# Moving layer 1's last adaLN products from its attention stage into layer 0's dense stage

## The chip, the cores and the metric

The kernel runs on one core of one Trainium2 chip. The metric is device time in microseconds. The core has a matrix engine (PE, TensorE), a vector engine (DVE, VectorE), a scalar engine (ACT, ScalarE), GpSimd (POOL) and a queue engine (SP) that in this kernel only issues DMAs. Each engine runs its own program in order; they meet through semaphores.

## The reference, cut to what matters

Two layers of a diffusion backbone, float32, over 256 latent and 256 context tokens of 1024 channels. Each layer takes six modulation vectors per stream out of one product, the adaLN product:

```python
def _adaln(cond, w, b):
    return jax.nn.silu(cond) @ w + b            # (1024,) @ (1024, 6144) + (6144,)

for l in range(2):
    sh1, sc1, g1, sh2, sc2, g2 = split(_adaln(c, ada_w[l], ada_b[l]), 6)      # latent stream
    csh1, csc1, cg1, csh2, csc2, cg2 = split(_adaln(c_ctx, ada_w[l], ada_b[l]), 6)   # context
    h = rms(x, norm1_w[l]) * (1 + sc1) + sh1    # and hc for the context
    ... attention, retention and convolution heads from h @ w_in[l] ...
    x = x + g1 * (concat(att, ret, cnv) @ w_out[l])
    h2 = rms(x, norm2_w[l]) * (1 + sc2) + sh2
    x = x + g2 * mixer(h2)    # layer 0: dense SwiGLU, width 2816; layer 1: top-2-of-8 experts, width 3584
```

The adaLN product depends on the conditions `c` and `c_ctx` alone, not on x, so it can be computed at any time before the vectors are used. In layer 1 the first two vectors are needed at its beginning, `g1` at its output projection, and the others behind that.

## The kernel before, in words

Matrix products of the layers are float32 accurate by three passes: a weight is split into a high and a low part in fp32r, and each product is high x high, high x low and low x high. A weight *item* of up to 1 MB is loaded by SP into one of `RAW` = 4 raw slots, ACT copies it into the high part (`split_to` on ACT, L1138), DVE subtracts for the low part (`split_to` on DVE, L1464), and PE multiplies by both (`three`, L519 to L521). A raw slot is free once DVE has made the low part (`lo_ready`); a parts slot is free once PE has used the item. The order of all loads is one list, `order_in`, built before the engines' programs and walked by SP at L1059 to L1082.

The adaLN weights are cut into 12 slices of 512 columns per layer and each slice into two halves of 1 MB, an *adaLN item*. An item is not split: `ada_product` (L525 to L538) multiplies it in plain float32 by the two conditions, in four matmuls that write four groups of 32 PSUM partitions. All products of a group of items add up in one bank. There are three groups. Group 0 (8 items, layer 0's first four slices) is multiplied at the start. Group 1 (24 items: the rest of layer 0, and layer 1's first four slices) is multiplied in layer 0's attention. Group 2 (16 items: layer 1's other eight slices) is multiplied in layer 1's attention. `ADA_ITEMS` says how many products PE does in each of the attention's iterations: for layer 1 it is 2, 3, 2, 3, 2, 2, 2 in the first seven of eight. These items are loaded into four slots, `ADA_SLOTS`: raw slots 0 and 1 and two buffers named `more`.

At the end of a group DVE copies the bank into SBUF (`ada_rows`, L1490, signals `rows_out`). PE *folds* it: eight small matmuls turn the rows into columns and add the bias (`fold_rows`, L548 and L549, signals `cols_full`). DVE copies the columns (`ada_columns`, L1495) and makes the scale of the second norm (`scale_columns`, signals `mod2_ready`). In both layers PE waits for `rows_out` at the first instruction of `project_out`, and folds after the first tile.

The attention is written as a pipeline of iterations `m` over pairs of heads: PE scores (L734), DVE masks and takes the maximum (L1706), ACT exponentials (L1215), PE transposes (L742), ACT copies (L1179), PE values (L753). DVE, ACT and GpSimd also work through the 31 taps of the convolution in it (L1692, L1202, L1440), five per iteration in layer 1.

Between the two layers stands layer 0's dense stage (`dense_ffn`), in two halves of 11 steps. Step f multiplies gate and up columns of one item (two loads of 512 KB) with all tokens: 48 matmuls of 512 columns. After the 11 steps of a half come six items of down weights. Items rotate through raw slots 0, 1, 2 and parts slots 0, 1, 2; raw slot 3 is not used there. ACT and DVE run through the same steps: in step f ACT takes the gate's activation (L1372), makes the high part of the hidden values of step f-1 (L1365), and then splits the item of step f+3; DVE likewise.

Of the kernel before, what the change touches and what calls it, by code (L numbers as in the profile page):

```python
# [28 lines left out]
RAW = 4  # L29
# [9 lines left out]
EARLY = 4  # L39
# [2 lines left out]
RO_TAP = (20, 13)  # L42
CONV_OUTS = 4
PRODUCTS = 4
ADA_ITEMS = ((2, 1, 2, 1, 2, 1, 2, 1, 2, 2, 2, 2, 2, 2, 0, 0), (2, 3, 2, 3, 2, 2, 2, 0))
ADA_SLOTS = (0, 1, RAW, RAW + 1)
TAPS = ((2, 3, 2, 3, 2, 3, 2, 3, 3, 3, 3, 2), (5, 5, 5, 5, 5, 5, 1))
READOUT = (5, 1)
# [61 lines left out]
def build(nc, io, place):  # L110
    ctx = ExitStack()
    with ctx:
# [59 lines left out]

        bank = [ctx.enter_context(nc.psum_tensor(f"bank{i}", [P, 512], F32)) for i in range(8)]
        VB, AB, OB = bank[0:4], bank[4:7], bank[7]
        rows_bank = (OB, VB[3], VB[3])

        def table(name):
            a, n = place[name]
# [102 lines left out]
        conv_full, conv_gone = sem("conv_bank_full"), sem("conv_bank_evacuated")  # L281
# [112 lines left out]
        for layer in range(DEPTH):  # L394
            if layer == 0:
                ada_items(0)
            first["in", layer] = len(items)
            n = 0
            for a, b in IN_SLICES:
                for k0, k1 in HALVES:  # L400
                    split_item([cols(io["w_in"][layer], a, b, k0, k1)], k1 - k0, b - a, n % 2, (n + layer) % 2)
                    n += 1
            ada_items(layer + 1)
            first["out", layer] = len(items)
            for h in range(2):
                for k0, k1 in HALVES:
                    split_item([cols(io["w_out"][layer], h * SLICE, (h + 1) * SLICE, k0, k1)],
                               k1 - k0, SLICE, n % 2, (n + layer) % 2)
                    n += 1
            if layer == 0:  # L410
                first["ffn"] = len(items)
                n = 0
                for p0 in range(0, FF_TILES, HALF_FF):

                    for f in range(p0, p0 + HALF_FF):
                        split_item([cols(io["ffn_w_gate"][0], f * P, (f + 1) * P), cols(io["ffn_w_up"][0], f * P, (f + 1) * P)],
                                   KT, 2 * P, n % 3, n % 3)
                        n += 1

                    for h in range(2):  # L420
                        for f0, f1 in ff_split:
                            split_item([io["ffn_w_down"][0][(p0 + f0) * P:(p0 + f1) * P, h * SLICE:(h + 1) * SLICE]
                                        .rearrange("(k p) n -> p k n", p=P)], f1 - f0, SLICE, n % 3, n % 3)
                            n += 1
                assert n % 3 == 1
# [32 lines left out]
        def _(pe):  # L458
# [93 lines left out]
            def turn_vectors():  # L552

                after(small_in, 16 * N_SMALL)
                nc.tensor.transpose(OB[:, 96:96 + 2 * KT + 2], vrows[:, :], ident[0:2 * KT + 2, 0:2 * KT + 2])\
                    .then_inc(vectors_full, 1)
# [249 lines left out]

            def project_out(layer):
                tiles = order_of(layer)
                after(rows_out)
                ring_v[0] = len(VB)  # L810
                for half in range(2):
                    outs = {}
                    for k0, k1 in HALVES:
                        n, hi, lo = next_item()
                        for i, t in enumerate(tiles):
                            if half == 0:
                                pe.wait_ge(mix_lo, mixed[layer, t, k0 // 4])
                            if t not in outs:
                                outs[t] = open_v()
                            tok = slice(t * P, (t + 1) * P)  # L820
                            for k in range(k0, k1):
                                mm = three(outs[t][:, :], (hTr[:, 0, k, tok], hTr[:, 1, k, tok]),
                                           (hi[:, k - k0, :], lo[:, k - k0, :]), k == 0, k == KT - 1)
                            if k1 == KT:
                                mm.then_inc(v_full, 1)
                            if k0 == 0 and i == len(tiles) - 1:
                                part_used(n, mm)
                            if half == 0 and k0 == 0:
                                if i == 0:
                                    after(att_read)  # L830
                                    turn_attended(layer, tiles[-1])
                                if i == len(tiles) // 2 - 1:
                                    turn_rest(layer)
                                    fold_rows(layer + 1)
                            if half == 0 and k0 and i == 0:
                                after(mod2_ready)
                                spread_gate(2, (0, 1) if layer == 0 else (0,))
                                job[("gates", layer)] = d_a[0] - 1
                    last_use[n] = (v_full, n_v[0])
                job[("mixed", layer)] = n_v[0]  # L840

            def dense_ffn():
                for p0 in range(0, FF_TILES, HALF_FF):
                    for f in range(p0, p0 + HALF_FF):
                        n, hi, lo = next_item()
                        for half in range(2):
                            b = open_a(("gate", f)) if half == 0 else open_v(("up", f))
                            c0 = half * P
                            for k in range(KT):
                                if f == 0 and half == 0 and k % (KT // 2) == 0:  # L850
                                    after(h_lo, KT // 2)
                                mm = three(b[:, :], (hi[:, k, c0:c0 + P], lo[:, k, c0:c0 + P]),
                                           (hTr[:, 0, k, :], hTr[:, 1, k, :]), k == 0, k == KT - 1)
                            mm.then_inc(a_full if half == 0 else v_full, 1)
                        last_use[n] = (v_full, n_v[0])
                    if p0 == 0:
                        spread_gate(5, (0, 1))
                        pe.wait_ge(a_done, d_a[0])
                    after(ff_lo, HALF_FF)
                    if p0:  # L860
                        turn_vectors()
                    for half in range(2):
                        outs = [open_v() for _ in range(NT)]
                        for f0, f1 in ff_split:
                            n, hi, lo = next_item()
                            for f in range(f0, f1):
                                for t in range(NT):
                                    tok = slice(t * P, (t + 1) * P)
                                    mm = three(outs[t][:, :], (HFr[:, 0, f, tok], HFr[:, 1, f, tok]),
                                               (hi[:, f - f0, :], lo[:, f - f0, :]), f == 0, f == HALF_FF - 1)  # L870
                                    if f == HALF_FF - 1:
                                        mm.then_inc(v_full, 1)
                            if f1 < HALF_FF:
                                part_used(n, mm)
                            else:
                                last_use[n] = (v_full, n_v[0])
# [173 lines left out]
        def _(sp):  # L1050
# [8 lines left out]
            for is_ada, n in order_in:  # L1059
                s = adas[n][3] if is_ada else items[n][3]  # L1060
                if is_ada and s == RAW:
                    sp.wait_ge(conv_full, CONV_OUTS * (1 if n < ADA_FIRST[2] else 2))
                if holder[s] is not None:
                    was_ada, before = holder[s]
                    sp.wait_ge(ada_used if was_ada else lo_ready, before + 1)
# [384 lines left out]
        def _(dve):  # L1450
# [228 lines left out]
            def attention(layer, base):  # L1679
# [16 lines left out]
                for m in range(last + 2):  # L1696
# [27 lines left out]
                    if m == last - 1:  # L1724
                        split_to(first["out", layer] + 2)
                    if m == last:
                        ada_rows(layer + 1)
                    if m % 4 == 1 and m >= 5:
                        turn = (m // 4 - 1) % 2
                        tile = order_of(layer)[m // 4 - 1]  # L1730
# [196 lines left out]
            for layer in range(DEPTH):  # L1927
# [22 lines left out]
                mix_low(layer, order_of(layer)[-1], 0)  # L1950
                for t in order_of(layer):
                    mix_low(layer, t, 1)
                ada_columns(layer + 1)
                scale_columns(1, mod2_ready, layer + 1)
                O = first["out", layer]
                for half in range(2):
                    split_to(O + 2 * half + 3 if half == 0 or layer == 0 else O + 4)
# [11 lines left out]
                if layer == 0:  # L1969
# [6 lines left out]
                    for p0 in range(0, FF_TILES, HALF_FF):  # L1976
# [10 lines left out]
                        hidden_low(p0 + HALF_FF - 1)  # L1987
                        if p0:
                            after(small_in, 16 * N_SMALL)
                            vectors()  # L1990
                            scale_columns(0, mod1_ready, 2)
                        for half in range(2):
                            for j in range(len(ff_split)):
                                if j == len(ff_split) - 1:
                                    for t in tiles:
                                        add_gated(half, t, p0 > 0 and half == 1)
                                n += 1
                                split_to(min(n, first["in", 1] + 2))
# [42 lines left out]
```

## Time and profile before

| | us |
|---|---|
| median of 3 runs | 2016.98 (2013.34 to 2017.33) |
| the profiled execution | 2017.29 |
| its span, first to last instruction | 2015.3 |
| PE busy | 1857.1 (92% of the span) |
| DVE busy | 1350.3 (67%) |
| ACT busy | 1036.7 (51%) |
| the chain of work that ended last, by engine | PE 78%, DVE 11%, DMA 5%, ACT 3% |

The span is one execution on one core. A busy share is an average over stages with different limits; the chain names, for each moment, the instruction that the end of the kernel stood waiting for. Layer 0's dense stage lies at about 372 to 750 us of the span, layer 1's attention at 863 to 918, and the experts from 987 to the end.

### The profile page before, as it was taken

How to read it: one execution, taken by the hardware profiler on the slowest of the kernel's cores; microseconds unless marked ns; L12 is line 12 of the kernel's file. 1: busy time of each engine (PE TensorE's matmuls, PEld its weight loads, DVE VectorE, ACT ScalarE, POOL GpSimd, SP SyncE). 2: the span in 40 equal slices, each digit the busy share in tenths (PEclk: the TensorE clock that was granted, in tenths of full speed). 3: DMA queues.
4: the chain of work that ended last, by engine and by line, in shares of the span. 5: the costliest groups of instructions: out<-in, count | busy, mean ns of one | idle time of the engine just before them, and what ended most of it. 6: DMA issues, size and time to landing. Idle time of an engine off the chain costs nothing.

```text
span 2015.3 us, 23614 instructions
## 1 busy us (share of the span) xinstructions
PE 1857.1 (92%) x8916; PEld 1499.9 (74%) x8916; DVE 1350.3 (67%) x1286; ACT 1036.7 (51%) x972; POOL 115.4 (6%) x127
## 2 busy tenths in 40 slices
PE   4899888799999987998699999999999999999997
PEld 1777457688788767857588888788887888878885
DVE  1464964432243225685698988989888888888886
ACT  2322542432122115263377776777767767667773
POOL 0021710100000000250000000000000000000000
PEclk9899989899999998998799999999999999999999
DMA  8223832432333112392499998999999999899994
GB/s 291 84 88 125 302 133 71 106 88 90 84 105 100 58 58 89 105 334 84 145 370 334 374 366 313 358 336 373 357 328 354 346 357 373 328 350 339 366 367 157
DMA packets 245914, 472.89 MB, mean 235 GB/s; under 512 B 10546, under 2 KB 60564, under 8 KB 245804
## 3 DMA queue, kind: packets, MB, share of 16 engines
q1 hardware_dynamic: 241856, 468.67, 65.5%
q10 hardware_dynamic: 3948, 2.67, 0.5%
q8 instruction: 79, 1.29, 0.3%
q14 instruction: 31, 0.25, 0.0%
HBM read 470.26 MB, written 1.05 MB: 234 GB/s over the span
## 4 chain that ended last, share of the span: by engine, by line
PE 78%; DVE 11%; DMA 5%; ACT 3%; issue 2%; POOL 1%; SPq 0%; ACTq 0%; DVEq 0%; POOLq 0%
PE bank L519 23%; PE bank L521 22%; PE bank L520 22%; DVE parts L1479 2%; DVE parts L1464 2%; PE bank L537 1%; PE bank L920 1%; DMA raw<-in_ada_w_dram 1%; PE bank L934 1%; ACT parts L1240 1%; PE bank L961 1%; DMA raw<-in_moe_w_gate_dram 1%; DMA raw<-in_moe_w_up_dram 1%; PE bank L753 1%; ACT parts L1138 1%
## 5 line engine op out<-in xcount | busy, mean ns | idle before, releaser
L1479 DVE TENSOR_TENSOR parts<-raw,parts 128x2048 fp32r<-128x2048 f32 x336 | 765.0, 2289 | 113.1 <-ACT parts L1240 112.0
L1240 ACT ACTIVATE parts<-raw 128x2048 fp32r<-128x2048 f32 x336 | 642.4, 1918 | 259.6 <-DMA raw<-in_moe_w_up_dram 90.1
L519 PE MATMUL bank<-parts,XEr 128*128 128x512 f32 x896 | 355.0, 396 | 7.7 <-DVE XEr L1479 3.9
L521 PE MATMUL bank<-parts,XEr 128*128 128x512 f32 x896 | 350.0, 391 | 0.0
L520 PE MATMUL bank<-parts,XEr 128*128 128x512 f32 x896 | 349.6, 390 | 0.0
L1138 ACT ACTIVATE parts<-raw 128x2048 fp32r<-128x2048 f32 (+1 forms) x62 | 113.3, 1831 | 331.1 <-PE bank L521 308.4
L1464 DVE TENSOR_TENSOR parts<-raw,parts 128x2048 fp32r<-128x2048 f32 (+1 forms) x62 | 135.4, 2188 | 194.1 <-ACT parts L1138 194.0
L519 PEld LDWEIGHTS bank<-parts,XEr 128*128 128x128 f32 x896 | 168.6, 188 | 43.4 <-DVE parts L1479 5.9
L521 PEld LDWEIGHTS bank<-parts,XEr 128*128 128x128 f32 x896 | 168.6, 188 | 35.8
L520 PEld LDWEIGHTS bank<-parts,XEr 128*128 128x128 f32 x896 | 168.8, 188 | 33.5
L519 PE MATMUL bank<-parts,HTr 128*128 128x512 f32 x448 | 180.8, 404 | 0.7 <-DVE parts L1479 0.7
L521 PE MATMUL bank<-parts,HTr 128*128 128x512 f32 x448 | 174.6, 390 | 0.0
L520 PE MATMUL bank<-parts,HTr 128*128 128x512 f32 x448 | 174.4, 389 | 0.0
L519 PE MATMUL bank<-hTr,parts 128*128 128x512 f32 (+1 forms) x416 | 160.7, 386 | 5.3 <-DVE parts L1464 2.1
L521 PE MATMUL bank<-hTr,parts 128*128 128x512 f32 (+1 forms) x416 | 158.6, 381 | 0.0
L520 PE MATMUL bank<-hTr,parts 128*128 128x512 f32 (+1 forms) x416 | 158.6, 381 | 0.0
L519 PE MATMUL bank<-parts,hTr 128*128 128x512 f32 (+1 forms) x320 | 124.3, 389 | 18.5 <-DVE hTr L1479 8.6
L521 PE MATMUL bank<-parts,hTr 128*128 128x512 f32 (+1 forms) x320 | 122.4, 382 | 0.0
L520 PE MATMUL bank<-parts,hTr 128*128 128x512 f32 (+1 forms) x320 | 122.2, 382 | 0.0
L1479 DVE TENSOR_TENSOR HF<-bank,SG 128x512 f32<-128x512 f32 x22 | 15.2, 692 | 145.4 <-PE bank L521 145.4
L519 PEld LDWEIGHTS bank<-parts,HTr 128*128 128x128 f32 x448 | 84.1, 188 | 22.0 <-issue 3.3
L520 PEld LDWEIGHTS bank<-parts,HTr 128*128 128x128 f32 x448 | 84.2, 188 | 20.3 <-issue 3.3
(220 smaller groups left out, 2319.0 us busy)
## 6 DMA issues: line engine op xcount, KB each, us to landing
raw<-in_moe_w_gate_dram SPq DMA_DIRECT2D x112, 1024.0 KB, 7.0
raw<-in_moe_w_up_dram SPq DMA_DIRECT2D x112, 1024.0 KB, 7.2
raw<-in_moe_w_down_dram SPq DMA_DIRECT2D x112, 1024.0 KB, 6.6
raw<-in_ada_w_dram SPq DMA_DIRECT2D x28, 1024.0 KB, 7.8
more<-in_ada_w_dram SPq DMA_DIRECT2D x20, 1024.0 KB, 7.5
raw<-in_w_in_dram SPq DMA_DIRECT2D x12, 1024.0 KB, 5.4
raw<-in_ffn_w_gate_dram SPq DMA_DIRECT2D x22, 512.0 KB, 4.0
raw<-in_ffn_w_up_dram SPq DMA_DIRECT2D x22, 512.0 KB, 5.3
```

What stands on the lines that cost most here:

```text
L519: nc.tensor.matmul(out, st[0], mv[0], start=start, stop=False)
L520: nc.tensor.matmul(out, st[0], mv[1], start=False, stop=False)
L521: return nc.tensor.matmul(out, st[1], mv[0], start=False, stop=stop)
L537: mm = nc.tensor.matmul(b[32 * j:32 * j + 32, :], cond[:, half * KT // 2 + j, c0:c0 + 32], w[:, j, :], start=opening, stop=closing)
L753: mm = nc.tensor.matmul(OB[:, head * 64:(head + 1) * 64], PT[:, n % 4, kb * P:(kb + 1) * P], proj[:, kb, C_V + 64 * g:C_V + 64 * g + 64], ...
L920: mm = nc.tensor.matmul(M[k // 4][:, (k % 4) * P:(k % 4 + 1) * P], xn[:, t, k * P:(k + 1) * P], PA[:, t, bass.ds(i * 2 + j, 1), :].rearran ...
L934: nc.tensor.matmul(M[h][:, :], SCAT[:, ee % 2, t * P:(t + 1) * P], YS[:, h * 512:(h + 1) * 512], start=True, stop=True).then_inc(scatter_f ...
L961: mm = nc.tensor.transpose(T[g % 2][:, j * P:(j + 1) * P], HE[:, g % 2, j * P:(j + 1) * P], ident)
L1138: nc.scalar.activation(parts[:, s, 0, 0:k * width], raw[:, r, 0:k * width], ACT.Copy).then_inc(hi_ready, 1)
L1240: nc.scalar.activation(parts[:, n % PARTS, 0, :], raw[:, r, :], ACT.Copy).then_inc(hi_ready, 1)
L1464: nc.vector.tensor_tensor(parts[:, s, 1, 0:k * width], raw[:, r, 0:k * width], parts_f[:, s, 0, 0:k * width], ALU.subtract).then_inc(lo_re ...
L1479: return nc.vector.tensor_tensor(out, a, b, op)
```

## The change

The 16 items of group 2 leave layer 1's attention. One stands behind each of the steps f = 2 to 17 of the dense stage, in the order of loads and in PE's program, and all go through raw slot 3. Their products add up in bank 7 (`OB`) instead of bank 3. Row copy, fold, columns and the second scale follow in the second half of the dense stage, in front of its down products.

```diff
-ADA_ITEMS = ((2, 1, 2, 1, 2, 1, 2, 1, 2, 2, 2, 2, 2, 2, 0, 0), (2, 3, 2, 3, 2, 2, 2, 0))
+ADA_ITEMS = ((2, 1, 2, 1, 2, 1, 2, 1, 2, 2, 2, 2, 2, 2, 0, 0), (0,) * 8)
+ADA_IN_FFN = range(2, 18)
-        rows_bank = (OB, VB[3], VB[3])
+        rows_bank = (OB, VB[3], OB)
   # order of loads
-            ada_items(layer + 1)
+            if layer == 0:
+                ada_items(1)
...
                         n += 1
+                        if f in ADA_IN_FFN:
+                            ada_item(1, EARLY + ADA_IN_FFN.index(f) // 2, ADA_IN_FFN.index(f) % 2, RAW - 1)
   # PE, project_out
-                after(rows_out)
+                if layer == 0:
+                    after(rows_out)
...
-                                    fold_rows(layer + 1)
+                                    if layer == 0:
+                                        fold_rows(1)
   # PE, dense_ffn
                         last_use[n] = (v_full, n_v[0])
+                        if f in ADA_IN_FFN:
+                            ada_product()
...
                     after(ff_lo, HALF_FF)
                     if p0:
+                        after(rows_out)
+                        fold_rows(2)
                         turn_vectors()
   # SP
                 if is_ada and s == RAW:
-                    sp.wait_ge(conv_full, CONV_OUTS * (1 if n < ADA_FIRST[2] else 2))
+                    sp.wait_ge(conv_full, CONV_OUTS)
+                if is_ada and n == ADA_FIRST[2]:
+                    sp.wait_ge(v_full, job[("mixed", 0)])
   # DVE, attention, project_out and the dense stage
                     if m == last:
-                        ada_rows(layer + 1)
+                        if layer == 0:
+                            ada_rows(1)
...
-                ada_columns(layer + 1)
-                scale_columns(1, mod2_ready, layer + 1)
+                if layer == 0:
+                    ada_columns(1)
+                    scale_columns(1, mod2_ready, 1)
...
                         if p0:
                             after(small_in, 16 * N_SMALL)
+                            ada_rows(2)
                             vectors()
+                            ada_columns(2)
                             scale_columns(0, mod1_ready, 2)
+                            scale_columns(1, mod2_ready, 2)
```

SP's rule for a slot stays as it is: before a load into a slot that an adaLN item holds it waits until PE has multiplied that item (`ada_used`).

## Rows read from the trace of the kernel before

**Rows 1.** Chain of waits, layer 1's attention: start us, us, what; x counts instructions
```profile
869.17 4.34 PE bank L537 x24
...
884.06 7.81 DMA more<-in_ada_w_dram
...
902.90 1.85 PE bank L537 x16
...
917.25 0.58 DVE row L1490
```

**Rows 2.** Windows, all engines: window, length, busy us (instructions) each, clock, DMA, GB/s
```profile
863.90:905.80 41.90, 38.66 (x281) 20.07 (x273) 35.88 (x79) 30.75 (x74) 26.45 (x32) 0.96 0.99 356
```

**Rows 3.** Timeline of DVE, 863 to 922: start, us, line, operation [idle before <-releaser]
```profile
887.79 0.69 DVE L1706 CUSTOM_DVE_ANT_0 SC<-bank,mask 128x512 f32<-128x512 f32 x1 [1.10 <-issue]
...
905.85 0.69 DVE L1706 CUSTOM_DVE_ANT_0 SC<-bank,mask 128x512 f32<-128x512 f32 x1 [3.53 <-PE bank L734]
...
917.16 0.66 DVE L1490 COPY row<-bank 128x512 f32<-128x512 f32 x1
...
920.89 0.69 DVE L1479 TENSOR_TENSOR proj<-bank,rsum 128x512 f32<-128x512 f32 x1
```

**Rows 4.** Timeline of ACT, end of layer 1's attention
```profile
909.88 3.70 ACT L1138 ACTIVATE parts<-raw 128x2048 fp32r<-128x2048 f32 x2
```

**Rows 5.** Timeline of PE, layer 1's attention and output projection
```profile
867.83 1.34 PE L742 MATMUL bank<-const,SC 128*128 128x128 f32 x8 [1.98 <-ACT SC L1215]
...
923.16 0.83 PE L721 MATMUL bank<-const,proj 128*128 128x128 f32 x4
...
924.71 0.29 PE L548 MATMUL bank<-const,row 128*128 128x16 f32 x2
...
926.86 0.47 PE L549 MATMUL bank<-const,biasr 24*128 24x16 f32 x2
```

**Rows 6.** Windows of three microseconds: second to last columns clock, DMA share, GB/s
```profile
870.00:873.00 3.00, 3.00 (x24) 0.68 (x16) 2.89 (x4) 3.00 (x9) 2.46 (x4) 0.59 0.50 136
...
683.00:686.00 3.00, 2.74 (x7) 2.22 (x8) 0.56 (x3) 0.00 (x0) 0.00 (x0) 0.50 0.70 212
```

**Rows 7.** Timelines of ACT, then DVE, in two steps of the dense stage
```profile
392.39 1.92 ACT L1138 ACTIVATE parts<-raw 128x2048 fp32r<-128x2048 f32 x1 [4.38 <-PE bank L521]
...
403.27 1.92 ACT L1138 ACTIVATE parts<-raw 128x2048 fp32r<-128x2048 f32 x1 [4.38 <-PE bank L521]
...
394.34 2.29 DVE L1464 TENSOR_TENSOR parts<-raw,parts 128x2048 fp32r<-128x2048 f32 x1 [0.72 <-ACT parts L1138]
```

**Rows 8.** L1076, first loads of step 6: issues, and time from issue to landing
```profile
L1076 SPq DMA_DIRECT2D raw<-in_ffn_w_gate_dram x1: 367/367/367, 385.8 to 385.8; - x1
L1076 SPq DMA_DIRECT2D raw<-in_ffn_w_up_dram x1: 585/585/585, 386.2 to 386.2; - x1
...
DMA to landing us min/median/max: 4.0/4.6/5.2
```

**Rows 9.** SP's timeline 346 to 350, then L1076's landings from 347.2 to 350
```profile
346.47 0.37 SPq L1076 DMA_DIRECT2D raw<-in_ffn_w_gate_dram  x1
...
348.69 1.57 SPq L1076 DMA_DIRECT2D raw<-in_ffn_w_up_dram  x1
...
DMA to landing us min/median/max: 5.3/6.5/7.1
```

**Rows 10.** L1068, 835 to 870: landing of adaLN items; then a window in the experts
```profile
DMA to landing us min/median/max: 5.1/5.4/7.6
...
1000.00:1050.00 50.00, 50.00 (x227) 41.35 (x226) 42.62 (x24) 38.67 (x27) 0.00 (x0) 1.00 0.90 335
```

**Rows 11.** Timeline of PE, ends of the dense stage's two halves
```profile
490.05 3.96 PE L803 MATMUL bank<-const,ada 128*128 128x128 f32 x32
494.69 0.50 PE L519 MATMUL bank<-parts,HFr 128*128 128x512 f32 x1 [0.69 <-ACT gb L1179]
...
683.26 0.29 PE L555 MATMUL bank<-const,vrows 18*128 18x18 f32 x1 [4.03 <-DVE HFr L1479]
```

## The prediction, made before the changed kernel was run

> **What bounds the kernel now.** I read the page first: PE is busy for 92% of the span and carries 78% of the chain, so PE time added where PE never idles is paid in full. Next I read the chain inside layer 1's attention, where the change takes work away. It names the adaLN products seven times, 24 records in 4.34 us first and 16 in 1.85 us last, 12.0 us in sum over the seven pieces, and one DMA wait of 7.81 us for adaLN weights [rows 1]. Read alone, this says that products and loads hold the attention by 19.8 us. So the third view was DVE's timeline there, because a chain shows one of several ways that end together. Of the 41.9 us from DVE's first mask to its last, DVE is busy 35.9 [rows 2], and only two idle pieces in it are longer than 0.1 us: 1.10 and 3.53 us [rows 3]; the rest of the difference is latency between dependent taps. From 864 to 887 it never stops. The products fill PE's gaps under DVE's work. Last I read the dense stage. A step repeats every 10.88 us (ACT's splits at 392.39 and 403.27, [rows 7]), which is 48 matmuls without a gap between them: there PE alone sets the time. The change moves work from under DVE's cover to where nothing covers it.
>
> **The products, added.** 16 products of 4 matmuls. Two products (16 records) take 1.85 us of chain [rows 1], so 0.93 each at the full clock. In the dense stage each stands alone between fp32r matmuls, and I take 1.0: 16.0 us. Below, 0.93 each gives 14.9. Above, 0.3 for the two changes of form around each gives 20.8.
> The Trainium skill (TensorEngine Tiling (Array Packing), Key Properties) says that changing the tiling mode drains TensorE, which speaks against products scattered one by one, since there are 32 changes where attention had fewer. The trace has two products in 1.85 us with such changes at both ends, so a drain can't be large there; the upper bound above already holds one.
>
> **The weights of the dense stage, late.** This is the term that the PE rows do not show. In the order of loads an adaLN item now follows the items of f = 2 to 17, all in slot 3, so SP waits before each for the product before it. Everything behind it in SP's program waits too. The adaLN item behind load f waits for the product behind step f-1; load f+1 stands behind it. So load n is issued only after step n-2 and its product, where before it was issued once the low part of item n-3 was made (SP at 385.77 for item 6, just after DVE's split in step 0) [rows 8]. Held loads are 4 to 10, the first down item, and 13 to 18; loads 11 and 12 are issued during the down products.
> From the end of that product to the item being ready: SP 0.05; the adaLN item and then 1 MB of gate and up. Gate and up alone land 5.6 us after the first issue (0.4 between the issues, then 5.2) [rows 8]. One MB more in front takes 3.1 us at 335 GB/s [rows 10], so 8.7; the adaLN issue is itself hidden, and I take 8.6. Then 0.1 to wake ACT, its split 1.92, DVE's 2.29 [rows 7], 0.1 of semaphores. Sum 13.06. Until PE needs the item it has one step and one product, 10.88 + 1.0 = 11.88. The item is 1.2 us late. A late item n delays step n, and load n+2 hangs on step n's product, so the lateness returns every second step: steps 4, 6, 8, 10 and 13, 15, 17, seven times, 8.1 us. Bounds of the landing: 6.0, as if the adaLN MB did not delay the other (nothing late, 0 us), and 9.3, from four loads of 512 KB issued at 346.47 to 348.69, the last landing 7.1 after its issue [rows 9], other small loads among them (1.9 late, 13 us).
> The Trainium skill (DMA: Bandwidth & Descriptors, Measured) gives 6.15 us for a DMA of 1 MB. By it two would take 12.3 us, the item would come 4.9 us late and the sum would grow by 26 us. The adaLN items here land within 5.1 us of issue, issue and latency included [rows 10], so I don't follow it.
>
> **Between the halves.** Before, PE starts the down products 4.64 us after the last step of the first half (490.05 to 494.69), most of it the gate spreading [rows 11]. Now ACT and DVE are behind, since in step 8 both were blocked for the first down item until about 10 and 12.5 us after the product of step 9. From there DVE has three hidden products and low parts (0.7 us each), and two more splits (2.3 and 1.8): the last low part is there at about 20 us, that is 8.0 after the end of step 10 (10.88 + 1.2 after the same product). Against 4.64 + 1.0 this is 2.4 more. PE idles over 3 us in it. After the idle of 4.03 us at 679 [rows 11] the clock stood at 0.50 [rows 6], and some matmuls at half rate add 0.6. I take 3.0; bounds 0 and 6.
>
> **Second half: rows and fold.** PE waits at 683.26 for DVE's last low part [rows 11]. Now DVE copies the rows next (0.66) [rows 3] and PE folds, eight matmuls from 924.71 to 927.33, 2.6 us less 0.3 of overlap [rows 5]. 0.7 + 2.3 + 0.3 for a longer cold start is 3.3; bounds 2.6 and 4.5. DVE's column copies and scales, under 1 us, lie under the down products. The queue past them is free: no load waits there.
> Sum added: 16.0 + 8.1 + 3.0 + 3.3 = 30.4 us.
>
> **Layer 1's attention, removed.** Without products the scores of a pair come as soon as values are done. DVE's wait of 1.10 goes. Of the 3.53 most goes, but next come ACT's taps and copies, and GpSimd's last tap, which ended 0.2 us before PE turned the convolution; I let the whole pipeline come 3.1 earlier at ACT's split, now at 909.88 [rows 4]. That split (3.70) and DVE's (4.49) remain. The row copy before the attended tile's scaling (0.66) goes. PE no longer waits for the rows, so its first tile starts some 5 us earlier, but its next instruction needs DVE's scaling at 920.89 [rows 3]: what is late next is that DVE chain, 3.1 + 0.66 + the POOL wait unchanged. So the turn at 923.16 [rows 5] comes about 4.5 earlier, since 0.9 of PE's own time stood between. The fold's 2.3 go, but 0.5 returns as the wait for the next tile's low part, which the fold hid. 4.5 + 1.8 = 6.3. Against that, PE is left with under two thirds of its work in the attention, and there it already fell to 0.59 of full clock at 870, after 1.98 us of idle before 867.83 [rows 5, 6]. At half rate PE has about 7.6 us of work per iteration (scores, turns, values at twice their 3.8) against DVE's 6.2, so it can push for a stretch: 1.0 back. Gain 5.3; bounds 0 and 9. The loads of the output weights no longer stand behind adaLN loads, but their split stands at a fixed place in ACT's program, so this is worth nothing. The DMA traffic moved is hidden in either place except as priced above.
>
> **Sum.** 30.4 - 5.3 = +25.1 against the profiled execution's 2017.29 (span 2015.3 and 2.0 around it): 2042.4. The profiled execution lies 0.3 above the median of 2016.98, so I predict 2042.
>
> **Rivals.**
> A, the chain is right (faster). Attention gives back all that the chain names: 19.8, the row copy 0.6 and the fold 2.3, 22.7 us. The dense stage costs only its lower bounds, 14.9 + 2.6 = 17.5, because loads are still in time: 5.2 less than the median, 2011.8. It decides if attention gives over 17.5 us plus whatever the loads are late. For it speaks the 7.81 us DMA wait, against it the unbroken DVE timeline before it.
> B, loads in time, but attention held by DVE. The landing is under 7.4 us after SP is released, so the item is ready before PE; then 16.0 + 3.3 + 0 to 2 between the halves, less 5.3: 2031. For it speak 4.0 us for 512 KB alone; against it 335 GB/s as the rate of a stream.
> C, loads later and the clock lost. Landing 9.3 (13 us), products at 1.2 (19), between halves 5, second half 4.5, and PE's halved clock makes it the limit of the attention, eight iterations of 1.4 us more, which eats the gain: 41.5 - 0, 2058.
> D, the change does nothing that can be told: dense PE time has slack I don't see, or gains equal costs, 2017. Against it: PE without a gap in the step.
>
> **How the numbers follow.** Forecast 0.46 (2035 to 2050), A 0.09, B 0.24, C 0.17, D 0.04. Within 0.2% (4 us), about what a measurement of this kernel can tell, holds D and the near part of A: same 0.05. Faster 0.08. Slower 0.87. The range for 8 in 10 leaves out A and D (0.13) and the far part of C: 2025 to 2057. The bounds of the terms alone, all low, 14.9 + 0 + 0 + 2.6 - 9, give +8.5, and all high 20.8 + 13 + 6 + 4.5 - 0, +44.3.
>
> **What would show it.** In the changed profile: products in the dense stage at 0.9 to 1.1 us each and full clock. SP's gate loads each issued within 0.1 us behind a product, from load 4 on. ACT's splits in the dense stage waiting for a DMA instead of for PE, and PE waiting about 1.2 us for DVE's low part in every second step (steps 4, 6, 8, 10). A longer idle of PE before the first down products. A fold between 680 and 720. In layer 1's attention no L537, DVE nearly unbroken over some 38 us, and the clock partly at half. It would be wrong if dense steps with a product stayed at 11.9 us throughout (then B), or if the attention from first scores to the first output matmul shrank by more than 10 us (then towards A).

## The result and the profile after

The changed kernel takes 2055.83 us (2051.45 to 2057.43, 4 runs) against 2017.15 us for the kernel before: ratio 1.0192, 95% interval 1.0171 to 1.0213, slower. Forecast were 2042, in a range of 2025 to 2057. The time lies at the upper end of the range, outside the 2035 to 2050 that the forecast itself stood for, and nearer to rival C (2058). The direction and the places were right, the terms of cost were too small.

The profiled execution has a span of 2054.7 us, 39.4 more than before. Cut at the same events in both traces, it comes from here:

| stretch | before | after | difference |
|---|---|---|---|
| start to the dense stage's first step | 372.96 | 371.63 | -1.3 |
| steps 0 to 10 | 117.1 | 136.2 | +19.2 |
| end of step 10 to the first down matmul | 4.6 | 7.7 | +3.1 |
| down products and steps 11 to 21 | 184.5 | 202.0 | +17.4 |
| end of step 21 to the first down matmul | 4.3 | 9.1 | +4.9 |
| down products to DVE's first mask in layer 1 | 180.5 | 180.3 | -0.2 |
| first mask to ACT's split of the output weights | 45.9 | 46.2 | +0.3 |
| that split to DVE's last normalised tile | 43.6 | 38.6 | -5.0 |
| the rest | 1061.8 | 1063.0 | +1.1 |

Experiments are read in the same cuts; the expert stage alone differs by 1 us and more between executions of equal code (1027.0 to 1035.2 us from its first gather in the profiles of this study), so small differences of totals say little, and the cuts before it say more.

The term that no PE row of before showed is there. This is the chain of waits of the changed kernel from the product behind step 2 on (start us, us, what):

```profile
401.84 1.04 PE bank L541 x8
402.90 0.37 SPq L1080
403.31 0.51 SPq L1088
403.87 8.82 DMA raw<-in_ffn_w_up_dram
412.71 1.93 ACT parts L1150
414.66 2.30 DVE parts L1476
```

SP's load of the adaLN item goes out 0.02 us after the product ends, the gate and up loads of step 4 behind it, and they land 9.8 us after that first issue; over the 13 held loads of gate and up it is 9.2 to 10.2 us until ACT starts on them. Before, ACT's split of that item had begun at 392.39 [rows 7]. ACT's row of the changed kernel says what it waited for now (columns as in [rows 7]), and PE's rows what that costs:

```profile
412.71 1.92 ACT L1150 ACTIVATE parts<-raw 128x2048 fp32r<-128x2048 f32 x1 [26.03 <-DMA raw<-in_ffn_w_up_dram]
```
```profile
401.77 1.06 PE L541 MATMUL bank<-raw,cond 128*32 128x512 f32 x8
413.88 1.07 PE L541 MATMUL bank<-raw,cond 128*32 128x512 f32 x8
417.00 0.79 PE L523 MATMUL bank<-hTr,parts 128*128 128x512 f32 x1 [2.06 <-DVE parts L1476]
429.73 1.06 PE L541 MATMUL bank<-raw,cond 128*32 128x512 f32 x8
441.84 1.07 PE L541 MATMUL bank<-raw,cond 128*32 128x512 f32 x8
444.41 0.50 PE L523 MATMUL bank<-hTr,parts 128*128 128x512 f32 x1 [1.51 <-DVE parts L1476]
```

Two things are to be read off. Product to product without a wait is 12.11 us (401.77 to 413.88), and a bare step was 10.88, so a product costs 1.23 us, not its 0.93 and not my 1.0. And the step that starts at 417.00 takes 12.73 us up to its product, where the one from 444.41 with its product's start at 455.56 takes 11.15: after the wait of 2.06 us the clock fell, which the window shows (columns as in [rows 2]). Behind the longest of these waits, 2.31 us, it did not fall:

```profile
417.00:420.00 3.00, 3.00 (x7) 2.42 (x8) 1.15 (x2) 0.00 (x0) 0.00 (x0) 0.51 1.00 352
```
```profile
673.71 0.50 PE L523 MATMUL bank<-hTr,parts 128*128 128x512 f32 x1 [2.31 <-DVE parts L1476]
```
```profile
676.00:679.00 3.00, 3.00 (x15) 2.49 (x14) 3.00 (x4) 1.92 (x1) 0.00 (x0) 1.00 1.15 308
```

The largest waits of PE in the dense stage of the changed kernel, in sum, times, and longest:

```profile
PE bank L523 <- DVE parts L1476: 13.9, 11, 2.3
PE bank L523 <- DVE YG L1491: 5.9, 2, 2.9
PE bank L552 <- DVE row L1502: 4.7, 1, 4.7
PE bank L807 <- ACT gb L1191: 1.9, 1, 1.9
```

The first line is new. The second was there before with the same 5.9. The fourth is new too and lies between the halves, where PE waits for ACT to spread the gate. The third answers to the idle of 4.03 us in [rows 11]; behind it the fold stands, at half clock:

```profile
722.27 0.58 PE L552 MATMUL bank<-const,row 128*128 128x16 f32 x2 [4.72 <-DVE row L1502]
...
726.00 0.60 PE L553 MATMUL bank<-const,biasr 24*128 24x16 f32 x2
```
```profile
722.00:725.00 3.00, 2.73 (x11) 2.57 (x11) 0.12 (x1) 0.00 (x0) 0.00 (x0) 0.50 0.71 261
```

In layer 1's attention no product is left and no DMA wait, and it is not shorter. Its last wait is even longer than the 3.53 us in [rows 3]. DVE first, then PE:

```profile
949.16 0.69 DVE L1718 CUSTOM_DVE_ANT_0 SC<-bank,mask 128x512 f32<-128x512 f32 x1 [4.23 <-PE bank L738]
```
```profile
942.62 3.65 PE L757 MATMUL bank<-proj,PT 128*128 128x64 f32 x16 [0.83 <-DVE proj L1491]
946.05 1.06 PE L725 MATMUL bank<-const,proj 128*128 128x128 f32 x4
947.05 2.08 PE L738 MATMUL bank<-AKT,heads 64*128 64x512 f32 x4
```

DVE has to scale a tile's attention before PE may write the next tile's values into the same bank, and only behind these values and a turn come the scores that DVE waits for. Two products (1.85 us) stood in that chain before. Now they are gone, but the values take 3.65 us, where they take 1.90 at the full clock. So this stretch is not evidence that the two products cost nothing; e6 and e7 come back to it.

### The profile page after: what moved, and what is told of

It reads as the page before. It is cut to its first block, busy times and chain, and to the rows that moved or that the text cites. A ratio compares the mean times of both kernels' runs of the same rounds, so it can differ in the third digit from the quotient of the medians.

```text
span 2054.7 us, 23559 instructions
## 1 busy us (share of the span) xinstructions
PE 1875.9 (91%) x8916; PEld 1506.6 (73%) x8916; DVE 1349.5 (66%) x1286; ACT 1034.7 (50%) x972; POOL 115.2 (6%) x127
## 4 chain that ended last, share of the span: by engine, by line
PE 64%; DVE 15%; DMA 11%; ACT 5%; issue 3%; POOL 1%; SPq 1%; ACTq 0%; DVEq 0%; POOLq 0%
PE bank L523 19%; PE bank L525 18%; PE bank L524 18%; DMA raw<-in_ffn_w_up_dram 4%; DVE parts L1491 4%; DMA raw<-in_moe_w_gate_dram 3%; DVE parts L1476 3%; ACT parts L1252 2%; DMA raw<-in_moe_w_down_dram 2%; ACT parts L1150 2%; DVE gb L1704 2%; DMA raw<-in_moe_w_up_dram 1%; PE bank L930 1%; DMA raw<-in_ada_w_dram 1%; PE bank L541 1%
## 5 line engine op out<-in xcount | busy, mean ns | idle before, releaser
L523 PE MATMUL bank<-hTr,parts 128*128 128x512 f32 (+1 forms) x416 | 163.3, 393 | 19.2 <-DVE parts L1476 16.0
L523 PE MATMUL bank<-parts,hTr 128*128 128x512 f32 (+1 forms) x320 | 122.4, 382 | 19.0 <-DVE hTr L1491 9.1
L525 PE MATMUL bank<-parts,hTr 128*128 128x512 f32 (+1 forms) x320 | 121.0, 378 | 0.0
L524 PE MATMUL bank<-parts,hTr 128*128 128x512 f32 (+1 forms) x320 | 120.6, 377 | 0.0
L523 PEld LDWEIGHTS bank<-hTr,parts 128*128 128x128 f32 x416 | 78.6, 189 | 50.1 <-DVE parts L1476 27.2
L524 PEld LDWEIGHTS bank<-parts,HTr 128*128 128x128 f32 x448 | 84.2, 188 | 20.3 <-issue 3.3
```

The lines of the kernel that those rows point to most:

```text
L523: nc.tensor.matmul(out, st[0], mv[0], start=start, stop=False)
L524: nc.tensor.matmul(out, st[0], mv[1], start=False, stop=False)
L525: return nc.tensor.matmul(out, st[1], mv[0], start=False, stop=stop)
```

## The experiments

**e1: adaLN loads three items later.** Order of loads only.

```diff
-                        if f in ADA_IN_FFN:
-                            ada_item(1, EARLY + ADA_IN_FFN.index(f) // 2, ADA_IN_FFN.index(f) % 2, RAW - 1)
+                        ada_due(n)    # item i behind weight item q(f_i) + 3, the products unmoved
```

> The changed kernel, with each adaLN load placed three weight items later in the order of loads; products stay where they are, nothing is left out. Theory 1 (SP held by the product before, in front of the next step's weights): PE's 11 waits for DVE's low part in the dense stage (13.9 us in sum) and the cold stretch behind the first (1.6) go, the gap between the halves shrinks by some 1.5; products still cost 1.23 us each. 2055.8 - 16.5 = about 2039. Rival (the products themselves, or 16 MB more traffic, delay the steps): the waits stay, 2053 or more.

Measured: 2033.84 us, ratio to before 1.0095 (1.0078 to 1.0112). Before was 2015.07 on that chip, so 18.8 us over before where the change was 38.7. PE's waits in the dense stage (all kinds over 0.4 us):

```profile
PE bank L529 <- DVE YG L1497: 5.9, 2, 2.9
PE bank L558 <- DVE row L1508: 4.7, 1, 4.7
PE bank L529 <- ACT gb L1197: 0.7, 1, 0.7
PE bank L529 <- DVE hTr L1497: 0.5, 1, 0.5
```

The line with 13.9 us has no successor, and the products stand 12.11 us apart throughout:

```profile
403.07 1.06 PE L547 MATMUL bank<-raw,cond 128*32 128x512 f32 x8
415.18 1.07 PE L547 MATMUL bank<-raw,cond 128*32 128x512 f32 x8
```

So 20 us of the 38.7, half of the loss, hung on where SP's loads stood in a list, with the same bytes, products and slot. By the two intervals this difference is uncertain by some 5 us, so the medians alone don't set it apart from the 16.5 expected. The cuts agree with 20: from step 0 to the second down products e1 is 20.3 us shorter. The gap between the halves went back to 4.5 us behind the product, and the half clock behind that gap, 1.6 us, which the expectation left out, is gone as well. The attention was 1.6 us shorter here than in the changed kernel, of which e5 and e6 tell more.

**e2: no group 2 at all.** Its items are neither loaded nor multiplied, rows set to zero, fold kept.

```diff
-ADA_IN_FFN = range(2, 18)
+ADA_IN_FFN = range(0)
```

> The changed kernel with the 16 adaLN items of group 2 neither loaded nor multiplied anywhere (their rows are set to zero, so layer 1's gates, second shift and scale hold the bias alone); rows, fold and columns stay in the dense stage. Theory 1 (layer 1's attention is held by DVE, so removing the products there is worth only what the tail gives, some 5 us, which the fold in the dense stage eats): 2016 to 2019, the same as before. Rival (the chain of waits of the kernel before is right, products and adaLN loads held the attention by 19.8 us): 1998 to 2001.

Measured: 2015.91 us, ratio 1.0006 (0.9995 to 1.0017), the same as before. 16 MB of loads and 16 products taken out of the kernel altogether, and it is no faster. First mask to last mask in layer 1's attention is 42.2 us, as in the changed kernel to 0.1, and 41.9 before. The total alone would not show this, since e2 also has two terms of the change that cancel, the later fold (4.8) and the shorter tail (5.0); the cut does. The 19.8 us that the chain of before gives to products and loads [rows 1] gave back nothing here, and rival A is out. But PE's clock was at half in iteration 6 of e2 as well, so what their removal is worth at full clock is read from e6.

**e3: the hold alone.** As e2, and SP waits as the adaLN items made it wait.

```diff
+                if 4 <= q <= 11:
+                    sp.wait_ge(v_full, job[("up", q - 2)] + 1)    # likewise for steps 13 to 18
```

> As e2, and SP waits for the end of PE's step n-2 before it loads the weights of step n (4 to 10, the first down item, 13 to 18), as the adaLN items made it wait. No adaLN load and no product. Theory 1 (hold and the MB in front add up; alone the landing of 5.6 us and the splits of 4.4 fit under the step of 10.88): no wait of PE over 0.3 us, within 1.5 us of e2. Rival (the hold alone makes the items late): PE waits in the dense stage, 5 to 13 us more than e2.

Measured: 2017.61 us, ratio 1.0012 (1.0002 to 1.0021), 1.7 us over e2, which the two intervals don't tell from nothing. PE's wait for late weights is one of 0.2 us:

```profile
PE bank L523 <- DVE parts L1481: 0.2, 1, 0.2
PE bank L807 <- ACT gb L1196: 1.9, 1, 1.9
```

The second line is the gap between the halves, where ACT and DVE were behind. It was not in the expectation, and neither were the 1.6 us that the clock cost behind it, as in the changed kernel; the steps were as expected. In the steps the hold by itself uses up the slack but no more.

**e9: hold and loads, without products.** The changed kernel, the loads released by the end of the step instead of the product; no product, rows zero.

```diff
-                        if f in ADA_IN_FFN:
-                            ada_product()
...
+                    if is_ada and n > ADA_FIRST[2]:
+                        sp.wait_ge(v_full, job[("up", n - ADA_FIRST[2] + 1)] + 1)
...
```

> The changed kernel with its 16 adaLN loads in place, each held until PE ends the step that the product before it stood behind, but no product is multiplied (rows are zero). So hold and added MB, without PE's own work. Theory (lateness is the landing behind one more MB, 9.8 us from the adaLN issue, and the splits, 4.4, against one step): with no product the slack is 10.9 instead of 12.1 us, so items come some 3 us late every second step: PE waits of 15 to 22 us in sum and, with cold stretches behind them and 2 us between the halves, 18 to 26 us over e2. Rival (it takes the products on PE to make the items late): waits under 5 us in sum.

Measured: 2047.55 us, ratio 1.0151 (1.0125 to 1.0176); against e2, each by its own kernel before, 29 us more, a little beyond the 18 to 26 expected. PE waits for weights 24.8 us in sum (15 to 22 expected), in eight waits; these are the first four:

```profile
415.76 0.50 PE L523 MATMUL bank<-hTr,parts 128*128 128x512 f32 x1 [3.13 <-DVE parts L1478]
442.41 0.50 PE L523 MATMUL bank<-hTr,parts 128*128 128x512 f32 x1 [2.97 <-DVE parts L1478]
467.55 0.50 PE L523 MATMUL bank<-hTr,parts 128*128 128x512 f32 x1 [3.08 <-DVE parts L1478]
494.62 0.50 PE L523 MATMUL bank<-hTr,parts 128*128 128x512 f32 x1 [3.39 <-DVE parts L1478]
```

This is the pattern of the prediction in its pure form, one wait every second step (4, 6, 8, 10), 3.1 us each, because the slack lacks the product's 1.2 us. Behind five of the eight waits the clock fell for 3.4 us. The 2 us expected between the halves did not come: that gap is 4.5 us, as in e2. Hold alone (e3) costs some 2, the added MB is what turns it into 29. That no product is needed for it shows that the lateness is one of loads.

**e4 and e5: PE's clock in layer 1's attention.** Four unused matmuls per group (operands on chip, unused bank). e4 puts one group in each iteration of the changed kernel; e5 puts 2, 3, 2, 3, 2, 2, 0, 0 into e1.

```diff
+                        for _ in range((1, 1, 1, 1, 1, 1, 1, 1)[m] if layer else 0):
+                            for j in range(KT // 2):
+                                nc.tensor.matmul(VB[3][32 * j:32 * j + 32, :], cond[:, j, 0:32], const[:, 0:512], start=True, stop=True)
```

> The changed kernel, with one group of four unused float32 matmuls (32x512, operands already on chip, into an unused bank) in each of the eight iterations of layer 1's attention. Theory 1 (the attention gained nothing from losing the products because PE's clock fell to half there): clock near 1.00, first mask to ACT's split of the output weights 43.0 us instead of 46.2, total 3 us less than the changed kernel, 2052.8. Rival (DVE and GpSimd set the length whatever the clock): 46 us, total unchanged or 1 to 5 us longer by the added PE work.

Measured: 2052.85 us, ratio 1.0184 (1.0167 to 1.0201), where the changed kernel's is 1.0192: nothing to tell. The trace is clearer, and the expectation missed: first mask to ACT's split took 47.4 us, not 43.0. The clock was near 1.00 for five iterations (but for 3.4 us early on), and DVE's masks came at the same offsets as in the changed kernel to 0.02 us up to iteration 6 (35.52 us after the first in both). So the rival holds for that part: DVE with GpSimd sets the pace whatever PE's clock. Then it fell just where it counts, with an unused group (0.93 us at full clock, 1.94 here) in the way as well:

```profile
947.82 3.68 PE L757 MATMUL bank<-proj,PT 128*128 128x64 f32 x16 [0.82 <-DVE proj L1494]
951.29 1.06 PE L725 MATMUL bank<-const,proj 128*128 128x128 f32 x4
952.28 1.94 PE L780 MATMUL bank<-const,cond 128*32 128x512 f32 x8
```

> e1 with unused matmuls in layer 1's attention, as many as the kernel before had products in iterations 0 to 5 (2, 3, 2, 3, 2, 2) and none in 6 and 7; e4 had held the clock at 1.00 up to iteration 5 but PE fell to half just when DVE waited for its scores in iteration 6. Theory (the one stretch where PE's clock counts is values, turn and scores of iteration 6): at full clock there, DVE's last mask comes 38.6 us after the first instead of 42.2 (after) or 40.6 (e1), and the total is 2 us under e1. Rival (the attention's length doesn't hang on the clock): no change against e1, or longer by the work added.

Measured: 2033.60 us, ratio 1.0093 (1.0069 to 1.0117), not to be told from e1. In the trace the values of iteration 6 ran at full clock, and DVE's last mask came 39.4 us after the first, against 40.6 in e1, 42.2 in the changed kernel and 43.4 in e4:

```profile
923.70 2.00 PE L763 MATMUL bank<-proj,PT 128*128 128x64 f32 x16 [0.72 <-DVE proj L1500]
925.53 0.61 PE L731 MATMUL bank<-const,proj 128*128 128x128 f32 x4
926.07 1.13 PE L744 MATMUL bank<-AKT,heads 64*128 64x512 f32 x4
```

The clock in this one stretch goes with up to 3 us. One profile each, and a total that doesn't resolve 1 us: the place is shown, a gain of the whole is not. Nor is it shown that the unused matmuls kept the clock up, as the next run tells.

**e6: e1, rows copied in step 18 and folded before PE's wait for the last low part.**

```diff
+                            if f == 18:
+                                ada_rows(2)
...
+                    if p0:
+                        after(rows_out)
+                        fold_rows(2)
                     after(ff_lo, HALF_FF)
```

> e1, and DVE copies the rows in step 18 of the dense stage and PE folds before it waits for the last low part, inside the idle of 4.0 us it has there. Theory (the second half's rows and fold cost 4.8 us because they stand behind that wait, half of it at half clock): 4 to 5 us under e1, and what is left over the kernel before is 16 products at 1.23 us (19.7) less the 5 us that the tail of the output projection gives, about +15. Rival (fold is on PE's path wherever it stands): 0 to 1 us under e1.

Measured: 2030.13 us, ratio 1.0067 (1.0042 to 1.0092), 3.7 under e1 by the medians, with intervals that overlap. In the cuts the gap before the second down products is 4.9 us shorter (4.2 against 9.1). The fold runs at full clock in what was idle, and of the wait 1.65 us is left:

```profile
697.41 0.29 PE L558 MATMUL bank<-const,row 128*128 128x16 f32 x2
...
699.56 0.39 PE L559 MATMUL bank<-const,biasr 24*128 24x16 f32 x2
701.60 0.23 PE L565 MATMUL bank<-const,vrows 18*128 18x18 f32 x1 [1.65 <-DVE HFr L1498]
```

What stays, 14.6 us over before by the medians (8.5 to 18.5 by the interval), compares with 16 products at 1.23 (19.7) less the 5.0 of the tail, 14.7. That it meets to 0.1 is chance: the attention, too, was shorter than before in this profile. Its code is that of e1, without any unused matmul, and yet PE had its full clock in iteration 6, DVE's last wait fell to 1.23 us, and its last mask came 39.2 us after the first (e1: 40.6, before: 41.9, changed kernel: 42.2):

```profile
919.09 0.69 DVE L1725 CUSTOM_DVE_ANT_0 SC<-bank,mask 128x512 f32<-128x512 f32 x1 [1.23 <-PE bank L744]
```

So at full clock the attention without products is 2.7 us shorter than before, and at half clock there it is not shorter at all. Which of the two a run gets is not settled by the code of the attention; why, no run shows.

**e7: the kernel before, two products moved from iteration 6 to 7, behind the convolution's turn.** In both layers that turn now stands in front of the products of its iteration.

```diff
-ADA_ITEMS = (..., (2, 3, 2, 3, 2, 2, 2, 0))
+ADA_ITEMS = (..., (2, 3, 2, 3, 2, 2, 0, 2))
```

> The kernel before; of layer 1's products the two of iteration 6 move to iteration 7, and in both layers the convolution's turn stands in front of the products of its iteration. Theory (only those two products stood on the path of the attention, in front of the scores that DVE waits 3.53 us for): DVE's last mask 1.8 us earlier, total 1 to 2 us less, near what can be measured. Rival (chain: every product counts, moved ones too): no change.

Measured: 2014.17 us, ratio 0.9995 (0.9978 to 1.0012), no change that can be told. The last mask came 41.0 us after the first instead of 41.9, half of what was expected. The wait in question fell from 3.53 us to 1.54, about as much as the two products take (1.85), but the one before it rose from 1.10 to 2.48:

```profile
904.89 0.69 DVE L1706 CUSTOM_DVE_ANT_0 SC<-bank,mask 128x512 f32<-128x512 f32 x1 [1.54 <-PE bank L734]
```

Inconclusive as a total. The profile shows one thing more. From ACT's split to the last normalised tile e7 takes 40.7 us and before 43.6, with the wait for the rows and the fold in the same places. The difference of 2.9 goes with PE's clock in the output projection, at the first tile's matmuls in before and then in e7:

```profile
918.00:922.00 4.00, 4.00 (x10) 3.13 (x11) 3.09 (x7) 0.63 (x1) 0.31 (x1) 0.50 0.83 308
```
```profile
920.00:924.00 4.00, 4.00 (x28) 3.60 (x26) 2.22 (x5) 2.12 (x4) 0.00 (x0) 0.99 0.16 57
```

**e8: e7, with rows, fold and columns inside the attention, in both layers.**

```diff
+                    if m == last:              # PE, attention; the fold goes to a bank of its own
+                        after(rows_out)
+                        fold_rows(layer + 1)
...
-                after(rows_out)                # PE, project_out
-                                    fold_rows(layer + 1)
...
                     if m == last - 1:          # DVE
+                        ada_rows(layer + 1)
                         split_to(first["out", layer] + 2)
                     if m == last:
-                        ada_rows(layer + 1)
+                        ada_columns(layer + 1)
+                        scale_columns(1, mod2_ready, layer + 1)
```

> e7, and in both layers DVE copies the rows before it splits the output weights, PE folds into a bank of its own inside the attention's last iteration, DVE copies columns there, and the output projection waits for no rows. All products stay in the attention. Theory (the change's whole gain lay in the tail of layer 1, 5 us, and is to be had without moving a product): 7 to 10 us under the kernel before, about 2007. Rival (the tail's gain needs the products gone, since rows come too late or the fold delays the values): within 2 us of e7.

Measured: 2002.92 us, ratio 0.9954 (0.9934 to 0.9974): faster, by 12.6 us in the medians and by 9.3 (5.2 to 13.3) in the ratio, so that it can't be told from the 7 to 10 expected; against the changed kernel it is some 50 us less. DVE copies the rows while it waits for ACT's split, and the columns between two steps of a norm:

```profile
898.19 0.69 DVE L1492 COPY row<-bank 128x512 f32<-128x512 f32 x1 [1.19 <-PE bank L537]
899.06 4.49 DVE L1466 TENSOR_TENSOR parts<-raw,parts 128x2048 fp32r<-128x2048 f32 x2 [0.18 <-ACT parts L1140]
...
904.41 0.19 DVE L1501 COPY ada<-bank 128x64 f32<-128x64 f32 x1
```

From the first mask to the last normalised tile layer 1 takes 82.9 us instead of 89.5, and layer 0 165.9 instead of 171.8. Of layer 1's 6.6 us, 4.5 lie in the tail behind the attention and 2.4 in the attention, where the last mask comes 39.5 us after the first with all 16 products still in it; the step between the two is 0.3 longer. Neither gain needs a product to leave the attention.

## Why the prediction came out as it did

- **The reading of the attention** (products lie under DVE's work) was right but for two of them; e2 shows it, against what the chain says, and e8 has 39.5 us from first to last mask with all 16 products in the attention, where e6 has 39.2 with none. That a chain with one long DMA wait and 12 us of products can be worth nothing, or 2.7 us at best, is the main lesson of this case.
- **The products**: direction right, size off. The term was 16 at 1.0, it measured 1.23: 19.7 instead of 16.0. The bound above (1.3) held. The 0.93 was read between neighbours of its own form; at a change to fp32r and back 0.3 comes on top. The drain at a change of tiling mode, of which the Trainium skill (TensorEngine Tiling (Array Packing), Key Properties) speaks, could explain it; no run separates it.
- **The weights, late**: mechanism right, and e1, e3 and e9 show each half of it. The size was too small, and it is the term that was missed by most. I took 8.6 us for the landing, and 9.2 to 10.2 were measured from the adaLN issue (9.8 at step 4). The row that I used as the upper bound [rows 9] had said 9.3, and it was the nearer one, since there too 2 MB were in flight. 13.9 us instead of 8.1. PE waits 11 times and not 7, at steps 4, 6 to 10, 13 to 16 and 18. I take this for no other mechanism, only one lateness split over neighbouring steps, 0.96 and 1.14 where e9 has one of about 3; step 18, with the longest wait of all (2.31), was not on my list.
- **The clock behind these waits** was not in the sum. After 2.06 us of idle in an otherwise gapless stage it fell, which cost 1.6 us (12.73 against 11.15). It fell behind one of the 11 waits, and not behind the longest.
- **Between the halves**: 3.0 expected beside the product, 0.6 of it for the clock. The gap grew by 1.8 (3.1 less 1.2), and the clock behind it cost 1.6: from the first down matmul to the wait for DVE's gated sum are 34.7 us, and 33.1 in the kernel before and in e1. 3.4 in sum, inside the bounds.
- **Rows and fold**: 3.3 expected, 4.9 measured. The copy delays PE by 0.7 as said, but the idle of 4.7 us before it put the fold at half clock, and it took 4.2 us instead of 2.3. The row of before that I priced it by [rows 5] was one at full clock, while [rows 6] already showed half a clock at this very place.
- **The attention**: the term said 3.1 less 1.0 for the clock. Measured 0 (0.3 us longer). The 3.1 were nearly right: at full clock e6 gains 2.7, and of DVE's wait of 3.53 us 2.3 were the two products, since 1.23 are left in e6; that rest is DVE's scaling, PE's values and the turn. What failed is the price of the clock: at half clock the same wait is 4.23, so 3.0 us were given back and not 1.0. Of the wait of 1.10, 0.7 was given back in the next iteration, where five taps took 4.09 us instead of 3.41.
- **The tail**: 4.5 less the above were expected to come mostly from the attention, and 1.8 from the fold; all 5.0 us came behind ACT's split. At most 2.1 of them are left for rows and fold. The other 2.9 are there in e7 too, with rows and fold in place, and go with PE's clock: in the kernel before it stood at half in the whole first output tile and part of the second. The total of the layer, 5.3, was right by luck, two errors that cancel.
- **Slips of reading** that moved little: the chain names the products six times, not seven (the 12.0 us are right); seven times 1.18 are 8.3 and not 8.1; and GpSimd's last tap ended 2.8 us before PE turned the convolution (905.64 and 908.41), not 0.2, so it held nothing there.
- **The rivals**: B is out, since the weights were late. C had what came: a landing of 9.3, products at 1.2, and an attention whose gain the clock eats; only its mechanism for that, PE's clock as the limit of all eight iterations, is not what the trace shows, where it counts in iteration 6 alone. It had a chance of 0.17. That the range holds the result owes much to this rival, and the centre of the forecast was 14 us too low.

Sum of the terms: 19.7 + 13.9 + 1.6 + 3.4 + 4.9 - 5.0 = 38.5; measured +38.7 in the medians and +39.4 in the profiles. The terms are read from the same profile, so that they add up shows that none is missing, and not that each has the cause given.

## What to carry to other kernels

Where an in-order queue engine serves several streams, a load that waits for a late consumer holds every load behind it: place it in the list by when its slot comes free, not by when it is used. Three places later in the list were worth 20 us here. A chain of waits names what was last, not what would remain: before moving work out of a stage, read the busy rows of the engine next in line over the whole stage, or run it once without the work. And small serial steps (row copy, fold, columns) should be looked for in idle stretches of their own stage before the bulk is moved to another one.

## What the runs showed of the hardware

- A group of four float32 matmuls on 32 columns costs 0.93 us next to its like [rows 1] and 1.23 between fp32r matmuls (12.11 less 10.88, changed kernel and e1).
- Two loads of 512 KB land 5.6 us after their first issue alone [rows 8]. With 1 MB issued 0.4 us before them they land 9.2 to 10.2 us after that MB's issue (13 cases in the changed kernel): 3.6 to 4.6 more, where the rate of the expert stage would give 3.1 [rows 10].
- PE's clock went to half after 2.06 us of idle in one place (417.00) and stayed at full after 2.31 in another (673.71); in e9 it stayed at full after 2.97 (442.41) and fell behind 2.85 (599.84). The idle's length alone didn't foretell it.
- Two kernels with the same code in the attention (e1 and e6) had different clocks there, and 40.6 and 39.2 us from first to last mask.
- DVE's taps, 0.50 us while GpSimd is idle or on a small tile, take 0.85 beside its adds on the same SBUF. The Trainium skill (GPSIMD Engine Reference, Specifications) says that the two share SBUF interfaces and contend when DVE has two SBUF inputs; the taps have two, and the trace agrees. This fits that removing a DVE wait of 1.1 us gave back only 0.4. The chain of the changed kernel shows both sizes, in iterations 3 and 4:

```profile
927.15 0.50 DVE gb L1704
...
932.52 0.84 DVE gb L1704
```
